# Layer 1's modulation with plain 4-byte products in place of split ones

## The chip, the cores and the metric

The kernel runs on one core of one Trainium2 chip. The metric is the device time of one launch, in microseconds (us): 5435.27 us is the median of three runs of the kernel before, which gave 5428.91, 5435.27 and 5438.29 us. Times inside the kernel come from one profiled execution of its own.

## What is computed

A backbone of two layers over 512 latent and 256 context tokens of width 1024. Each layer begins with a modulation: a conditioning vector (one for the latents, one for the context) is multiplied into a 1024 x 6144 weight matrix, and six vectors of 1024 (shift, scale and gate, twice) come out.

```python
cond_lat = jax.nn.silu(c)
cond_ctx = jax.nn.silu(c_ctx)
for l in range(DEPTH):
    mod_lat = (cond_lat @ w_mod[l] + b_mod[l])[:, None, :]
    mod_ctx = cond_ctx @ w_mod[l] + b_mod[l]
    sh1, sc1, gt1, sh2, sc2, gt2 = jnp.split(mod_lat, 6, axis=-1)
    h = _rmsnorm(x, g_norm1[l]) * (1.0 + sc1) + sh1
    p = h @ w_in[l]
    ...   # attention, short convolution, Hyena, merge, PEER experts
```

The Hyena branch needs a small filter network (two layers with sines) that depends on weights alone. Its first two steps are also computed during the modulation.

## The kernel before, in words

Every stage is a `Phase`: each engine has its own hand-written program, they meet through semaphores, and all engines wait for each other at the end of the stage. `phase_mod` (L764 to L919) is the stage of layer 1's modulation. It is the second stage of the program, after the load of the conditioning vectors, and nothing of another stage runs beside it. Layer 2's modulation is another function, `phase_mod_beside`, which runs beside the experts and which the diff leaves alone.

The weights come in 24 blocks of 1 MB, called halves here: 12 chunks of 512 output columns, each in two halves of 4 tiles of 128 rows (n counts halves, q = n // 2 counts chunks).

- **SyncE (SP)** issues the loads (L811) into a ring `raw` of 7 buffers. From the eighth on it first waits until VectorE has split half n - 7. Behind halves 7 to 10 it also issues the loads of x (2 MB), ctx (1 MB), rope and consts (L813).
- **ScalarE (ACT)** rounds each landed half to the reduced 4-byte format (`hi`, 3 buffers, L828). Between the halves it copies each finished chunk of 512 sums from PSUM into `rows` (`keep`, L822), sums the squares of the six token tiles at n = 16 to 21 (L837), takes their root at n = 23 (L841), and takes the two sines of the filter network at n = 12 and n = 23 (L761). The copy of the last chunk, `keep(11)`, stands behind the second sine.
- **VectorE (DVE)** computes the remainder `lo` = weights - `hi` (3 buffers, `split`, L265). At n = 3 and n = 14 it makes the filter network's angles (L727). At the end it normalises the tokens (`xn`, L911), adds the bias to the turned sums (L913) and forms the scales (L918).
- **TensorE (PE)** multiplies, for each half, 4 tiles of `hi` and 4 tiles of `lo` with `cond4`, the conditioning split in the same way into 4 columns (L873). After every second half it turns one kept chunk from 4 rows into 128 rows with 4 small products (`turn`, L861). At n = 2 and n = 13 it makes the filter network's products (L718). The last turn waits for `keep(11)`. At the end it transposes the modulation (L885), which ACT copies (L846) and SP stores (L801).
- **GpSimd (POOL)** reduces the filter network's angles to within pi in nine instructions each time (L742 to L755), and does nothing else in the stage.

The order inside each engine's program is what the loops over n write out; there is no planner.

Of the kernel before, what the change touches and what calls it, by code (L numbers as in the profile page):

```python
# [24 lines left out]
ALU = mybir.AluOpType  # L25
ACT = mybir.ActivationFunctionType
AX = mybir.AxisListType

P = 128
# [233 lines left out]
def split(nc, eng, hi, lo, x):  # L263

    return eng.tensor_tensor(lo, x, hi.bitcast(F32), ALU.subtract)  # L265
# [498 lines left out]
def phase_mod(c, layer, lay):  # L764
# [6 lines left out]

    nc, io = c.nc, c.io
    HALF = KD // 2
    RAW = 7
    chunks = 6 * D // 512
    raw = c.own(24, RAW, HALF * 512)
    DEEP = 3
    hi = [c.rounded(at, HALF * 512) for at in (80, 88, 96)]
    lo = [c.rounded(at, HALF * 512) for at in (140, 148, 192)]
    rows, turned_rows = c.at(178, 2, 512), c.at(178, 2, P)  # L780
    sel = c.at(182, 2)
    xn, junk = c.at(116, NT, D), c.at(184, 2, D)
    SQUARES = 16
    with Phase(nc) as ph:
# [3 lines left out]
                                    (c.rope[:], io["rope"]), (c.consts[:], io["consts"])]  # L788
        mlp = FilterMlp(c, ph, layer, T_ALL, lay.mlp_at)
        w_landed = [ph.sem(f"w_landed{s}") for s in range(RAW)]  # L790
        w_split, hi_ready, halves_done, kept, turned, cols_in, cond_split, dve_done = (ph.sem(s) for s in (
            "weights_split", "high_ready", "halves_done", "rows_kept", "rows_turned", "cols_landed",
            "cond_split", "dve_steps"))

        mod_ready, mod_turned, rows_made, rows_stored = (ph.sem(s) for s in (
            "mod_ready", "mod_turned", "rows_made", "rows_stored"))
# [1 line left out]
        def keep_rows(sp):  # L798
            sp.wait_ge(rows_made, 1)
            for s in range(2):  # L800
                sp.dma_start(c.mod_rows[layer][s], turned_rows[0:N_MOD, s]).then_inc(rows_stored, 16)  # L801
            sp.wait_ge(rows_stored, 32)

        @ph.block.sync
        def _(sp):
            sp.dma_start(c.cols[:], io["cols"][layer]).then_inc(cols_in, 16)
            mlp.sync(sp)
            for n in range(2 * chunks):
                if n >= RAW:
                    sp.wait_ge(w_split, n - RAW + 1)  # L810
                sp.dma_start(raw[:, n % RAW], io["w_mod"][layer][n]).then_inc(w_landed[n % RAW], 16)  # L811
                if n >= RAW and x_loads:
                    sp.dma_start(*x_loads.pop(0)).then_inc(x_in, 16)  # L813
            keep_rows(sp)

        @ph.block.scalar
        def _(act):
            def keep(q):
                act.wait_ge(halves_done, 2 * q + 2)
                if q >= 2:  # L820
                    act.wait_ge(turned, q - 1)
                nc.scalar.activation(rows[0:4, q % 2], c.bank(q % 2, 512, 4), ACT.Copy).then_inc(kept, 1)  # L822

            for n in range(2 * chunks):
                act.wait_ge(w_landed[n % RAW], 16 * (n // RAW + 1))
                if n >= DEEP:
                    act.wait_ge(halves_done, n - DEEP + 1)
                nc.scalar.activation(hi[n % DEEP], raw[:, n % RAW], ACT.Copy).then_inc(hi_ready, 1)  # L828
                if n >= 3 and n % 2:
                    keep((n - 3) // 2)  # L830
                if SQUARES <= n < SQUARES + NT:
                    t = n - SQUARES
                    if layer == 0 and t == 0:
                        act.wait_ge(x_in, 64)
                    if t >= 2:
                        act.wait_ge(sq, t - 1)
                    nc.scalar.activation(junk[:, t % 2], c.xs[:, t], ACT.Square,  # L837
                                         accum_out=c.stat[:, 0, t:t + 1]).then_inc(sq, 1)
                if n == SQUARES + NT + 1:
                    act.wait_ge(ms, 1)  # L840
                    nc.scalar.activation(c.stat[:, 1, 0:NT], c.stat[:, 1, 0:NT], ACT.Sqrt).then_inc(root, 1)  # L841
                if n in (12, 23):
                    mlp.scalar(act, n // 23, lay.hidden)
            keep(chunks - 1)
            act.wait_ge(mod_turned, 2)
            nc.scalar.activation(turned_rows[0:N_MOD], c.psum[0:N_MOD, 0:2 * P].rearrange("p (s q) -> p s q", s=2),  # L846
                                 ACT.Copy).then_inc(rows_made, 1)
# [7 lines left out]
        @ph.block.tensor  # L855
        def _(pe):
            def turn(q):
                pe.wait_ge(kept, q + 1)
                for j in range(4):
                    at = 7 * 512 + 8 * q + 2 * j  # L860
                    last = nc.tensor.matmul(c.psum[:, at:at + 2], rows[0:4, q % 2, j * P:(j + 1) * P], sel[0:4],  # L861
                                            start=True, stop=True)
                last.then_inc(turned, 1)

            pe.wait_ge(cond_split, 4)
            for n in range(2 * chunks):
                q, half = n // 2, n % 2
                if half == 0 and q >= 2:
                    pe.wait_ge(kept, q - 1)
                for part, ready in ((hi, hi_ready), (lo, w_split)):  # L870
                    pe.wait_ge(ready, n + 1)
                    for k in range(HALF):
                        last = nc.tensor.matmul(c.bank(q % 2, 512, 4), c.cond4[:, half * HALF + k],  # L873
                                                part[n % DEEP][:, k * 512:(k + 1) * 512],
                                                start=(half == 0 and part is hi and k == 0),
                                                stop=(half == 1 and part is lo and k == HALF - 1))
                last.then_inc(halves_done, 1)
                if n in (2, 13):
                    mlp.tensor(pe, n // 13)
                if n >= 3 and half:  # L880
                    turn((n - 3) // 2)
            turn(chunks - 1)
            pe.wait_ge(mod_ready, 2)
            for s in range(2):
                nc.tensor.transpose(c.psum[0:N_MOD, s * P:(s + 1) * P], c.mod[:, :, s], c.ident[:]).then_inc(mod_turned, 1)  # L885

        @ph.block.vector
        def _(dve):
            st = Steps(dve, dve_done)
            nc.vector.tensor_copy(c.cond4[:, :, 0:2], c.cond[:]).then_inc(cond_split, 1)  # L890
            dve.wait_ge(cond_split, 1)
            split(nc, nc.vector, c.cond4[:, :, 0:2], c.cond4[:, :, 2:4], c.cond[:]).then_inc(cond_split, 1)
            nc.vector.tensor_copy(sel[0:4], c.ident[0:4, 0:2]).then_inc(cond_split, 1)
            dve.wait_ge(cond_split, 3)
            nc.vector.tensor_tensor(sel[0:4], sel[0:4], c.ident[0:4, 2:4], ALU.add).then_inc(cond_split, 1)
            for n in range(2 * chunks):
                dve.wait_ge(hi_ready, n + 1)
                split(nc, nc.vector, hi[n % DEEP], lo[n % DEEP], raw[:, n % RAW]).then_inc(w_split, 1)
                if n == 3:
                    dve.wait_ge(cols_in, 16)  # L900
                if n in (3, 14):
                    mlp.vector(dve, n // 14)
                if n == SQUARES + NT:
                    dve.wait_ge(sq, NT)
                    nc.vector.tensor_scalar(c.stat[:, 1, 0:NT], c.stat[:, 0, 0:NT], 1.0 / D, EPS, ALU.mult,
                                            ALU.add).then_inc(ms, 1)
            dve.wait_ge(root, 1)
            st.do(nc.vector.reciprocal(c.stat[:, 0, 0:NT], c.stat[:, 1, 0:NT]))
            st.wait()
            for t in range(NT):  # L910
                nc.vector.tensor_scalar(xn[:, t], c.xs[:, t], c.stat[:, 0, t:t + 1], None, ALU.mult).then_inc(xn_ready, 1)  # L911
            dve.wait_ge(turned, chunks)
            st.do(nc.vector.tensor_tensor(  # L913
                c.mod[:], c.psum[:, 7 * 512:7 * 512 + 2 * N_MOD].rearrange("p (j s) -> p j s", s=2),
                c.cols[:, C_BMOD:C_BMOD + N_MOD].unsqueeze(2).to_broadcast([P, N_MOD, 2]), ALU.add))
            st.wait()
            for n, (sc, g) in enumerate(((SC1, C_G1), (SC2, C_G2))):
                nc.vector.scalar_tensor_tensor(  # L918
                    out=c.mod[:, sc:sc + KD] if n else c.ab[:], in0=c.mod[:, sc:sc + KD], scalar=1.0,  # L919
                    in1=c.cols[:, g:g + KD].unsqueeze(2).to_broadcast([P, KD, 2]), op0=ALU.add, op1=ALU.mult).then_inc(mod_ready, 1)  # L920
# [1919 lines left out]
```

## Time and profile before

| | |
|---|---|
| median of three runs | 5435.27 us |
| the profiled execution, its own time | 5433.36 us |
| its span, first to last instruction | 5431.3 us |
| mean granted TensorE clock over the span | 0.814 |
| busy share of the span: PE, DVE, POOL, ACT | 69%, 61%, 37%, 37% |
| the modulation stage of layer 1 in the span | 3.3 to 101.7 us |

The span is what the profile covers, from the first to the last instruction; the execution's own time is 2.1 us longer. A product of plain 4-byte operands shows up in the profile as two MATMUL records and two LDWEIGHTS records, one of reduced 4-byte operands as one of each. The granted clock is given as a share of 2.4 GHz: 1.00 is 2.4 GHz and 0.50 is 1.2 GHz.

### The profile page before, as it was taken

To read this page: it belongs to the slowest core of one execution; us is meant where nothing else is said; L and a number is where in the kernel's file an instruction comes from. 1 tells how busy PE (TensorE), PEld (TensorE's weight loads), DVE (VectorE), ACT (ScalarE), POOL (GpSimd) and SP (SyncE) were. 2 spreads that over 40 slices of the span, in tenths; PEclk is the share of its full clock that TensorE was granted. 3 is DMA by queue.
4 is the path that set the end of the run, shared out by engine and by line. 5 is a ranking of instruction groups with operands and counts; after the bars stand their busy time and mean duration, and the time that the engine had idled before them with its cause. 6 is when DMAs were issued, how large, how long until landed. Compare 5 with 4: busy or idle time off the path is not lost. (4 is left out here: it accounts for less than half of the span.)

```text
span 5431.3 us, 59703 instructions
## 1 busy us (share of the span) xinstructions
PE 3760.0 (69%) x19504; PEld 1838.0 (34%) x19504; DVE 3330.3 (61%) x7026; ACT 1988.8 (37%) x5136; POOL 2036.3 (37%) x1533
## 2 busy tenths in 40 slices
PE   6899879987565555555577679678976555555554
PEld 3677338876111111111122245246852111111111
DVE  7622452223777777777687777764135777777776
ACT  5432002212443344343354444325223443343443
POOL 5112003212444444444483356211434444444443
PEclk8999989998767777777688889889988777777777
DMA  5012002212999999999998989841327999999998
GB/s 237 16 44 70 4 16 65 63 67 103 400 418 410 416 410 417 415 414 414 378 363 349 367 327 375 349 171 37 98 80 325 421 412 417 413 415 416 411 417 345
DMA packets 230644, 1532.43 MB, mean 282 GB/s; under 512 B 26164, under 2 KB 26740, under 8 KB 58044
## 3 DMA queue, kind: packets, MB, share of 16 engines
q0 software_dynamic: 184320, 1342.26, 60.5%
q1 hardware_dynamic: 46012, 186.36, 9.4%
q8 instruction: 154, 2.52, 0.2%
q14 instruction: 158, 1.29, 0.1%
HBM read 1515.31 MB, written 13.21 MB: 281 GB/s over the span
## 5 line engine op out<-in xcount | busy, mean ns | idle before, releaser
L536 PE MATMUL psum<-arena 64*64 64x512 f32 x10240 | 1769.8, 825 | 1220.8 <-ACT arena L515 1209.6
L491 POOL DMA_INDIRECT arena<-in_uv,arena x1280 | 1462.9, 1143 | 1817.7 <-PE psum L536 1392.6
L651 DVE SCALAR_TENSOR_TENSOR arena<-arena 128x1024 f32<-128x1024 f32 x1280 | 1621.4, 1267 | 697.8 <-DMA arena<-in_uv,arena 653.0
L536 PEld LDWEIGHTS psum<-arena 64*64 64x64 f32 x10240 | 418.1, 169 | 2519.8 <-ACT arena L515 1892.9
L1549 PE MATMUL psum<-view_at,view_at 128*128 128x512 f32 (+1 forms) x4896 | 966.5, 359 | 19.1 <-PEq L165 10.3
L504 ACT ACTIVATE arena<-arena 128x1 f32<-128x1 f32 x1280 | 258.2, 202 | 1850.8 <-DVE arena L651 1811.0
L265 POOL TENSOR_TENSOR view_at<-view_at,view_at 128x1024 fp32r<-128x1024 f32 (+1 forms) x192 | 455.2, 2380 | 1238.7 <-ACT view_at L299 1208.4
L1549 PEld LDWEIGHTS psum<-view_at,view_at 128*128 128x128 f32 x4896 | 815.3, 191 | 185.2 <-issue 54.4
L515 ACT ACTIVATE arena<-arena 128x64 f32<-128x64 f32 x1280 | 445.1, 348 | 52.7 <-PE psum L536 10.9
L508 ACT ACTIVATE arena<-arena 128x1 f32<-128x1 f32 x1280 | 376.9, 294 | 46.7 <-ACT arena L504 0.4
L299 ACT ACTIVATE view_at<-view_at 128x1024 fp32r<-128x1024 f32 (+1 forms) x176 | 163.9, 939 | 330.6 <-DMA view_at<-in_w_in 188.2
L2405 DVE TENSOR_TENSOR view_at<-view_at,psum 128x768 f32<-128x768 f32 (+1 forms) x48 | 39.4, 821 | 376.2 <-PE psum L1549 376.2
L265 DVE TENSOR_TENSOR view_at<-view_at,view_at 128x2048 fp32r<-128x2048 f32 (+5 forms) x106 | 177.0, 1697 | 83.7 <-ACT view_at L2371 37.2
L2468 PE MATMUL psum<-view_at,view_at 128*128 128x512 f32 x480 | 114.5, 402 | 35.2 <-DVE view_at L265 34.1
L1269 PE MATMUL psum<-view_at,view_at 128*128 128x256 f32 (+1 forms) x528 | 96.7, 346 | 28.1 <-PEq L165 28.1
L2468 PEld LDWEIGHTS psum<-view_at,view_at 128*128 128x128 f32 x480 | 93.4, 195 | 56.0 <-issue 34.6
L504 ACT ACT_TABLE_LOAD x85 | 109.1, 1283 | 2.9 <-PEq L165 1.4
L1019 PE MATMUL psum<-view_at,cond 128*4 128x512 f32 x192 | 63.0, 466 | 64.8 <-POOL view_at L265 35.7
L651 DVE DVE_READ_ACCUMULATOR arena<-arena 128x1 f32 x1280 | 104.8, 82 | 0.0
L2240 PE MATMUL psum<-arena 128*128 128x256 f32 (+2 forms) x232 | 80.0, 511 | 34.6 <-DVE arena L2282 34.6
L558 DVE MAX8 arena<-arena 128x8 f32<-128x128 f32 (+1 forms) x240 | 81.5, 339 | 35.9 <-DVE arena L556 1.5
L472 ACT ACT_TABLE_LOAD x80 | 102.6, 1283 | 1.4
(246 smaller groups left out, 3445.6 us busy)
## 6 DMA issues: line engine op xcount, KB each, us to landing
view_at<-in_w_in SPq DMA_DIRECT2D x108, 512.0 KB, 6.6
view_at<-in_w_mod SPq DMA_DIRECT2D x48, 1024.0 KB, 12.9
arena<-in_uv,arena POOLq DMA_INDIRECT x1280
view_at<-in_w_br SPq DMA_DIRECT2D x48, 256.0 KB
view_at<-in_w_out SPq DMA_DIRECT2D x16, 512.0 KB, 8.7
view_at<-in_wq SPq DMA_DIRECT2D x16, 512.0 KB, 3.4
arena<-mod_rows SPq DMA_DIRECT2D x12, 512.0 KB
keep_spectrum<-arena SPq DMA_DIRECT2D x18, 256.0 KB, 6.9
```

The lines of the kernel that those rows point to most:

```text
L265: return eng.tensor_tensor(lo, x, hi.bitcast(F32), ALU.subtract)
L299: self._high(act, lambda out, x: self.c.nc.scalar.activation(out, x, ACT.Copy), n)
L472: self.c.nc.scalar.activation(self.exps[:, u % 2], self.topc, ACT.Exp, bias=self.small[:, u % 2, 0:1], accum_out=self.small[:, u % 2, 1:2] ...
L491: nc.gpsimd.indirect_dma_start(out=self.slots[i % self.ring], out_offset=None, in_=self.table, in_offset=bass.IndirectOffsetOnAxis(ap=self ...
L504: nc.scalar.activation(self.gelus[:, q, k:k + 1], self.dots[:, q, k:k + 1], ACT.Gelu).then_inc(self.act_steps, 1)
L508: nc.scalar.activation(self.scaled[:, q, k:k + 1], self.gelus[:, q, k:k + 1], ACT.Copy, scale=self.probs[:, q, k:k + 1]).then_inc(self.act ...
L515: nc.scalar.activation(self.diag[:, i % 4], self.ident2, ACT.Copy, scale=self.scaled[:, q, k:k + 1]).then_inc(self.diag_ready, 1)
L536: last = nc.tensor.matmul(self.c.psum[tokens, at:at + 512], self.diag[rows, k % 4], self.slots[k % self.ring][rows, D + h * 512:D + (h + 1 ...
L651: nc.vector.scalar_tensor_tensor(out=self.junk, in0=self.slots[i % self.ring][:, 0:D], scalar=1.0, in1=self.h2_turned if i % 2 else self.h ...
L1269: last = nc.tensor.matmul(out, h[:, k, at], m[:, lo:hi, k, :], start=(k == 0 and i == 0), stop=(k == KD - 1 and i == 2))
L1549: last = nc.tensor.matmul(c.psum[:, at + lo:at + hi], a[:, k], b[:, k, lo:hi], start=(k == 0 and i == 0), stop=(k == kt - 1 and i == 2))
L2468: last = nc.tensor.matmul(c.bank(2 * (t % 4) + h), a[:, k, t * P:(t + 1) * P], b[:, 4 * h:4 * h + 4, k, :], start=(k == 0 and i == 0), sto ...
```

## The change

The halves are no longer rounded and split. TensorE multiplies the landed 4-byte weights with the unsplit 4-byte conditioning, whose 2 columns replace the 4 of `cond4`. The ring is 10 buffers deep, SP waits for TensorE's products instead of VectorE's split, and the rows that are kept and turned are 2 instead of 4. The 48 instructions of rounding and splitting go away, as do the two that made `sel`. `cond4` is still made, for layer 2.

```diff
-    RAW = 7
+    RAW = 10
     chunks = 6 * D // 512
     raw = c.own(24, RAW, HALF * 512)
-    DEEP = 3
-    hi = [c.rounded(at, HALF * 512) for at in (80, 88, 96)]
-    lo = [c.rounded(at, HALF * 512) for at in (140, 148, 192)]
...
                 if n >= RAW:
-                    sp.wait_ge(w_split, n - RAW + 1)
+                    sp.wait_ge(halves_done, n - RAW + 1)
                 sp.dma_start(raw[:, n % RAW], io["w_mod"][layer][n]).then_inc(w_landed[n % RAW], 16)
...
-                nc.scalar.activation(rows[0:4, q % 2], c.bank(q % 2, 512, 4), ACT.Copy).then_inc(kept, 1)
+                nc.scalar.activation(rows[0:2, q % 2], c.bank(q % 2, 512, 2), ACT.Copy).then_inc(kept, 1)
 
             for n in range(2 * chunks):
-                act.wait_ge(w_landed[n % RAW], 16 * (n // RAW + 1))
-                if n >= DEEP:
-                    act.wait_ge(halves_done, n - DEEP + 1)
-                nc.scalar.activation(hi[n % DEEP], raw[:, n % RAW], ACT.Copy).then_inc(hi_ready, 1)
...
-                    last = nc.tensor.matmul(c.psum[:, at:at + 2], rows[0:4, q % 2, j * P:(j + 1) * P], sel[0:4],
+                    last = nc.tensor.matmul(c.psum[:, at:at + 2], rows[0:2, q % 2, j * P:(j + 1) * P], c.ident[0:2, 0:2],
                                             start=True, stop=True)
...
-            pe.wait_ge(cond_split, 4)
...
-                for part, ready in ((hi, hi_ready), (lo, w_split)):
-                    pe.wait_ge(ready, n + 1)
-                    for k in range(HALF):
-                        last = nc.tensor.matmul(c.bank(q % 2, 512, 4), c.cond4[:, half * HALF + k],
-                                                part[n % DEEP][:, k * 512:(k + 1) * 512],
-                                                start=(half == 0 and part is hi and k == 0),
-                                                stop=(half == 1 and part is lo and k == HALF - 1))
+                pe.wait_ge(w_landed[n % RAW], 16 * (n // RAW + 1))
+                for k in range(HALF):
+                    last = nc.tensor.matmul(c.bank(q % 2, 512, 2), c.cond[:, half * HALF + k], raw[:, n % RAW, k * 512:(k + 1) * 512],
+                                            start=(half == 0 and k == 0), stop=(half == 1 and k == HALF - 1))
                 last.then_inc(halves_done, 1)
...
             for n in range(2 * chunks):
-                dve.wait_ge(hi_ready, n + 1)
-                split(nc, nc.vector, hi[n % DEEP], lo[n % DEEP], raw[:, n % RAW]).then_inc(w_split, 1)
```

## Rows read from the trace of the kernel before

**Rows 1.** Groups of instructions by line, 0 to 110 us
```profile
L265 DVE TENSOR_TENSOR view_at<-view_at,view_at 128x2048 fp32r<-128x2048 f32 x24 | 58.8, 2472 | 21.5 <-ACT view_at L828 21.5
L873 PE MATMUL psum<-view_at,cond 128*4 128x512 f32 x192 | 54.2, 431 | 22.6 <-ACT view_at L828 15.7 <-DVE view_at L265 6.8
L828 ACT ACTIVATE view_at<-view_at 128x2048 fp32r<-128x2048 f32 x24 | 45.6, 1906 | 21.7 <-DMA view_at<-in_w_mod 20.9 <-PE psum L873 0.5
```

**Rows 2.** Busy time by stretch: PE, PEld, DVE, ACT, POOL, granted clock, DMA share, GB/s
```profile
10.00:35.00 25.00, 21.81 (x92) 8.55 (x92) 19.04 (x9) 16.76 (x12) 11.59 (x3) 1.00 1.01 425
35.00:52.00 17.00, 12.87 (x36) 4.30 (x36) 10.56 (x4) 10.47 (x7) 16.49 (x7) 0.60 1.01 417
52.00:76.00 24.00, 22.66 (x110) 9.97 (x109) 20.93 (x11) 21.97 (x22) 15.05 (x4) 1.00 0.95 395
76.00:94.00 18.00, 10.64 (x54) 4.74 (x53) 17.42 (x10) 10.81 (x13) 17.33 (x7) 0.95 0.00 0
```

**Rows 3.** Order of time, end of the stage: start, duration, engine, line
```profile
88.56 7.15 DVE L911 TENSOR_SCALAR arena<-arena,stat 128x1024 f32<-128x1024 f32 x6
...
93.87 0.84 ACT L761 ACTIVATE arena<-arena 64x768 f32<-64x768 f32 x1 [6.10 <-POOL arena L755]
94.62 0.57 ACT L822 ACTIVATE arena<-psum 4x512 f32<-4x512 f32 x1
...
95.25 1.86 PE L861 MATMUL psum<-arena 4*128 4x2 f32 x8 [4.69 <-ACT arena L822]
97.14 0.26 DVE L913 TENSOR_TENSOR mod<-psum,cols 128x96 f32<-128x96 f32 x1 [1.43 <-PE psum L861]
...
101.72 6.13 PE L1145 MATMUL psum<-ident,arena 128*128 128x128 f32 x36 [3.34 <-PEq L165]
```

**Rows 4.** GpSimd in order of time, the second reduction, first and last of nine
```profile
62.25 7.22 POOL L742 TENSOR_SCALAR arena<-arena 64x768 f32<-64x768 f32 x1 [8.78 <-DVE arena L727]
...
92.69 1.15 POOL L755 TENSOR_SCALAR arena<-arena 64x768 f32<-64x768 f32 x1
```

**Rows 5.** Order of time, 8 to 18 us: the first half arrives
```profile
10.22 1.91 ACT L828 ACTIVATE view_at<-view_at 128x2048 fp32r<-128x2048 f32 x1 [7.56 <-DMA view_at<-in_w_mod]
...
12.67 1.91 ACT L828 ACTIVATE view_at<-view_at 128x2048 fp32r<-128x2048 f32 x1 [0.54 <-DMA view_at<-in_w_mod]
...
17.03 0.12 PEld L873 LDWEIGHTS psum<-view_at,cond 128*4 128x4 f32 x1 [0.30 <-issue]
...
17.31 0.55 PEld L873 LDWEIGHTS psum<-view_at,cond 128*4 128x4 f32 x3 [0.15 <-issue]
```

**Rows 6.** TensorE and its weight loads at 574 us: plain 4-byte products, one stationary column
```profile
574.26 3.59 PE L1964 MATMUL psum<-arena,consts 128*1 128x512 f32 x8
...
575.97 0.08 PEld L1964 LDWEIGHTS psum<-arena,consts 128*1 128x1 f32 x1 [0.34 <-issue]
576.40 0.08 PEld L1964 LDWEIGHTS psum<-arena,consts 128*1 128x1 f32 x1 [0.35 <-issue]
```

**Rows 7.** TensorE at 521 us: a stretch that begins at the lower clock
```profile
521.44 3.33 PE L218 MATMUL psum<-ones,ident 128*128 128x128 f32 x14 [7.09 <-PEq L165]
525.26 7.16 PE L1945 MATMUL psum<-arena 64*128 64x512 f32 x8 [0.49 <-DMA arena<-in_hy_w]
```

**Rows 8.** Busy time by stretch, at and after the stretch of rows 7
```profile
527.00:533.00 6.00, 6.00 (x8) 2.16 (x7) 1.76 (x2) 3.57 (x5) 0.00 (x0) 0.50 0.96 412
536.00:540.00 4.00, 4.00 (x10) 1.50 (x10) 1.22 (x1) 0.70 (x1) 0.00 (x0) 1.00 0.02 8
```

**Rows 9.** TensorE in order of time, 59 to 71 us: halves, a filter product, turns
```profile
59.56 1.50 PE L718 MATMUL psum<-arena 64*64 64x512 f32 x4
60.99 1.05 PE L861 MATMUL psum<-arena 4*128 4x2 f32 x8
61.97 3.86 PE L873 MATMUL psum<-view_at,cond 128*4 128x512 f32 x16
...
66.74 3.86 PE L873 MATMUL psum<-view_at,cond 128*4 128x512 f32 x16
```

More of the change, by code:

```diff
@@ L773, in phase_mod @@
     HALF = KD // 2
-    RAW = 7
+    RAW = 10
     chunks = 6 * D // 512
     raw = c.own(24, RAW, HALF * 512)
-    DEEP = 3
-    hi = [c.rounded(at, HALF * 512) for at in (80, 88, 96)]
-    lo = [c.rounded(at, HALF * 512) for at in (140, 148, 192)]
     rows, turned_rows = c.at(178, 2, 512), c.at(178, 2, P)
-    sel = c.at(182, 2)
     xn, junk = c.at(116, NT, D), c.at(184, 2, D)
@@ L790, in phase_mod @@
         w_landed = [ph.sem(f"w_landed{s}") for s in range(RAW)]
-        w_split, hi_ready, halves_done, kept, turned, cols_in, cond_split, dve_done = (ph.sem(s) for s in (
-            "weights_split", "high_ready", "halves_done", "rows_kept", "rows_turned", "cols_landed",
-            "cond_split", "dve_steps"))
+        halves_done, kept, turned, cols_in, dve_done, cond_split = (ph.sem(s) for s in (
+            "halves_done", "rows_kept", "rows_turned", "cols_landed", "dve_steps", "cond_split"))
         mod_ready, mod_turned, rows_made, rows_stored = (ph.sem(s) for s in (
@@ L892, in _ @@
             split(nc, nc.vector, c.cond4[:, :, 0:2], c.cond4[:, :, 2:4], c.cond[:]).then_inc(cond_split, 1)
-            nc.vector.tensor_copy(sel[0:4], c.ident[0:4, 0:2]).then_inc(cond_split, 1)
-            dve.wait_ge(cond_split, 3)
-            nc.vector.tensor_tensor(sel[0:4], sel[0:4], c.ident[0:4, 2:4], ALU.add).then_inc(cond_split, 1)
             for n in range(2 * chunks):
-                dve.wait_ge(hi_ready, n + 1)
-                split(nc, nc.vector, hi[n % DEEP], lo[n % DEEP], raw[:, n % RAW]).then_inc(w_split, 1)
                 if n == 3:
```

## The prediction

> **What bounds the kernel now.** The change touches one stage, from 3.3 to 101.7 us of the span, so I read that stretch alone. The grouped lines come first [rows 1]: VectorE's 24 splits are busy 58.8 us, TensorE's 192 products 54.2 us, ScalarE's 24 roundings 45.6 us. None fills the stage's 98 us, so the table by stretch says who is ahead when [rows 2]. Until 76 us the DMA share is 0.95 to 1.01 at 395 to 425 GB/s: the transfers pace the stage, and the engines keep up but for a dip of TensorE, with a granted clock of 0.60, between 35 and 52 us. From 76 us on nothing moves (DMA 0.00), and VectorE (17.42 of 18 us) and GpSimd (17.33 of 18 us) are busy. So the last 18 us aren't the weights' transfer.
>
> The order of time at the end shows who closes the stage [rows 3]. ScalarE's second sine (L761) starts at 93.87 us, after waiting 6.10 us for GpSimd's last angle. Behind it stand the copy of the last chunk (94.62), the last turn on TensorE (95.25, 1.86 us long), the bias (97.14), and the next stage at 101.72. GpSimd's second reduction runs from 62.25 to 93.84 us, 31.6 us in nine instructions [rows 4]. The stage ends by this chain: weights until half 13, filter product, VectorE's angles, 31.6 us of GpSimd, sine, last chunk.
>
> **The change, part by part, and its sum.**
>
> What is removed: 58.8 us of VectorE and 45.6 us of ScalarE. Neither is worth anything by itself beyond the chain above: it is worth at most 101.7 us less the length of what takes its place. What takes its place is TensorE's stream, because a plain product costs more there.
>
> Price of a plain product. The profile has plain 4-byte products with 512 moving columns and a single stationary column: eight records in 3.59 us, weight loads 0.43 us apart (575.97 to 576.40) [rows 6]. Each product makes two records, so a product is 0.86 us and a half of four is 3.44 us. Two columns instead of one should cost the same; now a half is eight reduced records, 16 of them (two halves) in 3.86 us [rows 9], so 1.93 us. The step is from 1.93 to 3.44 us for each half, and a half arrives every 2.45 us (roundings of the first two halves start at 10.22 and 12.67 [rows 5], each waiting for a load). TensorE thus changes from faster than the transfers to slower than them.
>
> The Trainium skill, "Perfetto Trace Analysis", section "Engine Utilization", halves the array's output rate for FP32_LOW_HIGH. Taken for the whole product this would be 0.43 us a product, half the price that rows 6 show; taken for each record it agrees with them. The first reading is the faster rival below.
>
> Sum, in times of the span:
> - First product: the first half has landed at 10.2 us [rows 5]; today TensorE waits for the rounding, in future it doesn't.
> - 24 halves x 8 records x 0.43 us = 82.6 us.
> - Half rate at the begin. At 17.03 us a weight load still comes 0.42 us after the one before it (0.12 long, 0.30 idle), at 17.31 the idle time falls to 0.15 [rows 5]: the records go from 0.42 to some 0.24 us, so they ran at 1.2 GHz before, although the column says 1.00 there [rows 2]. That is 5 us after the first product, which follows the first rounding (10.22 + 1.91 = 12.1 us). Five microseconds at half rate lose 2.5 us. The other bound is the stretch at 521 us: TensorE begins at 521.44, a record still takes 0.9 us at 525 to 532 us (8 in 7.16), clock 0.50, and it is at 1.00 in the window from 536 [rows 7, 8]. Some 14.5 us, a loss of 7.2. I take 2.5, since that is this very stage with all 128 rows in use, where rows 7 have 64.
> - Ten turns before the last half ends. From a turn to the next product 0.98 us (60.99 to 61.97); from the pair's period, 4.77 us (61.97 to 66.74) less 3.86, it is at least 0.91 [rows 9]. With the tail of the last record under the turn I take 1.06: 10.6 us. Two rows instead of four change nothing: the cost is eight weight loads and eight tiny records.
> - Two filter products: 59.56 to 60.99, 1.43 us, with the gap ahead 1.5: 3.0 us.
> - Sum: 10.2 + 82.6 + 2.5 + 10.6 + 3.0 = 108.9; the copy of the last chunk starts at 109.1, against 94.62 today.
> - From that copy to the next stage today 101.72 - 94.62 = 7.1 us, of which the last turn is 1.86 at the low clock; on a TensorE just busy it is 1.05 [rows 3, 9]. So 6.3 us: next stage at 115.4, which is 13.7 us later.
> - The next stage starts with 36 transposes in 6.13 us at the lower clock [rows 3]. After a dense stream they may start fast. The first eight release VectorE, after which it is busy: between 0 and 2 us gained, I take 0.5.
>
> Together +13.2 us.
>
> What has to stay hidden. **Transfers:** half n needs its load by 10.2 + 2.5 + about 4.1 n us (3.44 and half a turn), and the queue delivers 1 MB in 2.45 us plus 3.1 MB of x, ctx, rope, consts (7.7 us) once; ten buffers hold 34 us of products, so SP's new wait for `halves_done` is never on the path. Behind it on SP stand only further loads. **GpSimd:** second filter product after half 13 at about 69 us, angles at 71, and even with today's 31.6 us [rows 4] it ends at 102.5. Without the splits beside it I expect it shorter. ScalarE comes to the second sine only after `keep(10)`, which needs half 21 (101) and the root, about 103.5; sine and tables end near 105.5, before 109. The first reduction has from 26 to 58 us even at 31.6 us, and TensorE asks for it behind half 13, at 67. **VectorE:** the root comes at 103.3 instead of 88, since it stands behind `keep(10)`; then the 7.15 us of `xn` [rows 3] end at 110.8, and the bias could start at 110.9. This is a tie: 0 to 0.5 us late.
>
> The profiled execution took 5433.36 us, so the changed kernel's would take 5446.6. The median of the runs, 5435.27 us, is 1.9 us higher; against it I forecast 5448.5 us. TensorE becomes the bound of the stage.
>
> **Rivals.**
> 1. No measurable change (chance 0.29). A measurement of this kernel can tell about 0.2%, 11 us, from no change, and the forecast is only 2 us above that. A quicker rise of the clock (loss 1 instead of 2.5), 2 us from transposes that start fast, or turns at 0.91 us (1.5 less) bring +8 to +11, some 5445. For it: the scatter of the three runs is 9 us. Against: these are small terms on 82.6 us that no view lets shrink.
> 2. Faster (0.07). If the two records of a product overlapped or were one for two columns, a half would cost 1.72 us, less than a load takes, and the transfers would pace the stage: half 13 lands at about 50, GpSimd runs from 55 to 86.5 at the old pace, the last copy starts at about 87.4 instead of 94.62. That with the warm turn is -8; with GpSimd freed of the splits up to -12, where `xn` closes the stage. Time about 5425. It decides below 2.5 us a half. Rows 6 with one column speak against it.
> 3. Much slower (0.04). If plain products with 2 of 128 columns don't hold TensorE at 2.4 GHz, each record is 0.86 us or more [rows 7]: the stream costs twice 82.6, turns 1.86 each, some +100 us, 5536. Rows 6 are eight records at the full rate, too short a burst to exclude it wholly; today's four columns do hold it [rows 2, 9].
> 4. The loads run dry in spite of the ring, as between 35 and 52 us today [rows 2]. At 2.45 us for a load against 3.44 for a half there is no way for it; it would only add to the forecast's side. I give it nothing of its own.
>
> **How the numbers follow.** Forecast (slower by over 0.2%) 0.60, rival 1 0.29, rival 2 0.07, rival 3 0.04. Slower is 0.60 + 0.04 = 0.64, same 0.29, faster 0.07. The range: down, quicker clock 1.5, transposes 1.5, turns 1.5, not all at once, and 4 us of run scatter give 5440; up, the 14.5 us rise (+4.7), the tie 0.5 and the same scatter give 5458. It leaves out rivals 2 and 3.
>
> **What the changed profile would show.** No 128x2048 instructions before 100 us on VectorE and ScalarE; L873's successor with 192 records, about 0.58 us each (3.59 less seven times 0.43 [rows 6]) and 0.43 us apart; TensorE without a gap over 1 us from 10.2 to about 109; the DMA share falling before 80 us or stretching as SP waits for TensorE; GpSimd's nine instructions in well under 31.6 us; the last copy on ScalarE waiting for TensorE, not sitting behind the sine; the next stage at about 115. Wrong would be a half in less than 2.5 us, or a granted clock of 0.50 in the middle of the stream, or a sine that starts after 109.

## The result and the profile after

The changed kernel takes 5451.23 us in the median of eight runs, the kernel before 5437.64 in the median of eight. The ratio is 1.0026 with a 95% interval of [1.0018, 1.0035], so the change costs 10 to 19 us. The forecast was +13.2 us against the median then shown (5448.5 from 5435.27); the measured difference of the medians is +13.6. That the two agree to 0.4 us is partly luck, since the interval is 9 us wide.

| | before | after |
|---|---|---|
| median of eight runs | 5437.64 us | 5451.23 us |
| profiled execution, own time | 5433.36 us | 5452.62 us |
| span | 5431.3 us | 5450.6 us |
| first product of the modulation | 12.28 us | 10.17 us |
| last chunk's copy (`keep(11)`) | 94.62 us | 109.16 us |
| first TensorE record of the next stage | 101.72 us | 115.60 us |

The grouped lines of the kernel after, 0 to 130 us (line, engine, operation, shapes, count | busy us, mean ns | idle before and its releaser), answer to [rows 1]:

```profile
L862 PE MATMUL psum<-view_at,cond 128*2 128x512 f32 x192 | 87.1, 608 | 10.2 <-DMA view_at<-in_w_mod 10.2
L749 POOL TENSOR_SCALAR arena<-arena 64x768 f32<-64x768 f32 x6 | 12.8, 2125 | 0.5
L742 POOL TENSOR_SCALAR arena<-arena 64x768 f32<-64x768 f32 x2 | 1.7, 827 | 52.9 <-DVE arena L727 52.9
L893 DVE TENSOR_SCALAR arena<-arena,stat 128x1024 f32<-128x1024 f32 x6 | 4.1, 749 | 0.0
```

There are still 192 records on TensorE, but they are busy 87.1 us instead of 54.2, and TensorE waits once, 10.2 us for the first load. The 24 roundings and the 24 splits are gone. The table by stretch of the kernel after (PE, PEld, DVE, ACT, POOL, granted clock, DMA share, GB/s) answers to [rows 2]:

```profile
16.00:35.00 19.00, 19.00 (x52) 4.48 (x51) 1.07 (x1) 1.17 (x2) 8.58 (x5) 1.00 1.03 430
35.00:52.00 17.00, 17.00 (x51) 4.56 (x49) 0.00 (x0) 1.17 (x2) 6.99 (x5) 1.00 1.00 413
52.00:76.00 24.00, 24.00 (x75) 7.07 (x75) 1.07 (x1) 3.53 (x6) 5.12 (x4) 1.00 0.95 394
76.00:94.00 18.00, 18.00 (x60) 5.39 (x58) 0.00 (x0) 6.04 (x12) 10.43 (x6) 1.00 0.00 1
```

TensorE is busy in every microsecond of these four stretches, at the full clock, also from 35 to 52 us where it had fallen to 0.60. The transfers end near 76 us as before; TensorE then has another 33 us to do. The order of time at the end of the stage answers to [rows 3]:

```profile
93.18 1.05 PE L852 MATMUL psum<-ident,arena 2*128 2x2 f32 x8
...
94.16 7.03 PE L862 MATMUL psum<-view_at,cond 128*2 128x512 f32 x16
...
101.12 1.05 PE L852 MATMUL psum<-ident,arena 2*128 2x2 f32 x8
...
103.59 4.07 DVE L893 TENSOR_SCALAR arena<-arena,stat 128x1024 f32<-128x1024 f32 x6
104.64 0.84 ACT L761 ACTIVATE arena<-arena 64x768 f32<-64x768 f32 x1
109.06 1.94 PE L852 MATMUL psum<-ident,arena 2*128 2x2 f32 x16
109.16 0.59 ACT L817 ACTIVATE arena<-psum 2x512 f32<-2x512 f32 x1 [3.67 <-PE psum L862]
111.04 0.26 DVE L895 TENSOR_TENSOR mod<-psum,cols 128x96 f32<-128x96 f32 x1 [3.38 <-PE psum L852]
...
115.60 7.01 PE L1127 MATMUL psum<-ident,arena 128*128 128x128 f32 x36 [3.33 <-PEq L165]
```

A pair of halves with its turn takes 7.94 us (93.18 to 101.12), where it took 4.77 [rows 9]. The sine (L761) is done at 105.5, and the last copy now waits 3.67 us for TensorE, not for GpSimd. The stage ends 13.9 us later (115.60 less 101.72).

The profiled span is 19.3 us longer, more than the stage explains. The rows of one large group in both kernels (minimum, median and maximum ns of one; first and last start in us), before and after, show where the rest is:

```profile
L1549 PE MATMUL psum<-view_at,view_at x4896: 277/389/793, 306.7 to 4098.6; 128*128 128x512 f32 x130, 128*128 128x256 f32 x66
```

```profile
L1531 PE MATMUL psum<-view_at,view_at x4896: 277/389/794, 318.7 to 4114.4; 128*128 128x512 f32 x130, 128*128 128x256 f32 x66
```

The shift is 12.0 us at 307 us of the span, 15.8 at 4099 and 19.3 at the end. The diff touches nothing there, and the eight runs of one kernel lie 13 to 16 us apart (5442.83 to 5455.65 after, 5428.91 to 5444.51 before). I read 5.4 of the 19.3 us as that scatter, which no single profile can resolve; the medians, 13.6 us apart, agree with the stage's 13.9.

### The profile page after: what moved, and what is told of

The parts are those of the page before. It is cut to its first block and busy times, and to the rows that moved or that the text cites. A ratio compares the mean times of both kernels' runs of the same rounds, so it can differ in the third digit from the quotient of the medians.

```text
span 5450.6 us, 59631 instructions
## 1 busy us (share of the span) xinstructions
PE 3781.2 (69%) x19504; PEld 1828.9 (34%) x19504; DVE 3266.7 (60%) x7000; ACT 1946.9 (36%) x5112; POOL 2009.3 (37%) x1533
## 3 DMA queue, kind: packets, MB, share of 16 engines
HBM read 1515.31 MB, written 13.21 MB: 280 GB/s over the span
## 5 line engine op out<-in xcount | busy, mean ns | idle before, releaser
L265 DVE TENSOR_TENSOR view_at<-view_at,view_at 128x512 fp32r<-128x512 f32 (+5 forms) x82 | 117.7, 1464 | 63.2 <-ACT view_at L2353 37.6
L504 ACT ACT_TABLE_LOAD x85 | 109.1, 1283 | 2.9 <-PEq L165 1.5
```

The costliest lines, as they stand in the source:

```text
L504: nc.scalar.activation(self.gelus[:, q, k:k + 1], self.dots[:, q, k:k + 1], ACT.Gelu).then_inc(self.act_steps, 1)
```

## The experiments

The landmark in all of them is the first TensorE record of the next stage: 101.72 us before, 115.60 after. Each kernel was profiled once, so how far the landmark scatters isn't measured in itself; the runs below give a measure. The first 24 records of the modulation took 13.21 us in the changed kernel and 11.99 in run 3, whose begin is the same. So a difference of about a microsecond between two landmarks tells nothing, where the whole time scatters by ten. The runs were made at four times, on three chips; each time the kernel before ran too, and whole times are compared only with that one.

**1. Half the products.** `for k in range(HALF)` becomes `for k in (0, HALF - 1)`; tiles 1 and 2 of each half are left out of the sums.

> The changed kernel with two of the four products of each half left out (tiles 1 and 2 of each half don't enter the sums). Theory, TensorE's stream sets the stage: the records go from 192 to 96, 41 us of stream go away, and the transfers take over: last half landed at about 75.5 us, root and xn behind it, next stage at about 86 us of the span instead of 115.6, some 29 us less in all (about 5422 us). Rival, the stage is held by latencies between the engines or by ScalarE's and VectorE's tail: the next stage stays above 105 us.

The order of time at the end of its stage:

```profile
74.38 1.88 PE L862 MATMUL psum<-view_at,cond 128*2 128x512 f32 x4
...
76.52 1.88 PE L862 MATMUL psum<-view_at,cond 128*2 128x512 f32 x4 [0.26 <-DMA view_at<-in_w_mod]
...
84.87 3.44 PE L1127 MATMUL psum<-ident,arena 128*128 128x128 f32 x15 [3.33 <-PEq L165]
```

The next stage starts at 84.87 us, 30.7 earlier (86 was expected), and now TensorE waits for the last load. So the stream set the stage, and the transfers stand behind it, 31 us lower. The whole took 5412.66 us, the kernel before beside it 5424.29, one run each.

**2. Five products instead of four.** The loop becomes `for k in (0, 1, 1, 2, 3)`; tile 1 enters the sums twice.

> The changed kernel with tile 1 of each half multiplied twice (it enters the sums twice), five products instead of four. Theory, TensorE's stream sets the stage at 0.86 us a product: 24 x 0.86 = 20.6 us more, next stage at 136 us. Rival, there is slack beside the stream: less than 10 us more.

```profile
135.48 0.87 PE L1127 MATMUL psum<-ident,arena 128*128 128x128 f32 x3 [3.33 <-PEq L165]
```

That is the first row of its next stage: 19.9 us later for 24 more products, 0.83 us each (0.86 expected, 20.6 in all). Of the missing 0.7 us 0.6 lie in a shorter stretch at half rate at the begin: its first 30 records took 15.17 us, where 13.21 us and six records of 0.43 make 15.79. There is no slack beside the stream. The whole took 5462.77 us against 5424.29.

**3. A ring of 3.** `RAW = 10` becomes `RAW = 3`.

> The changed kernel with a ring of 3 buffers instead of 10. Theory, the depth is worth nothing because a half of products (3.44 us) takes longer than a load (2.45 us): next stage at 115.6 to 118, with at most 3 us of waiting where the 2 MB of x pass between two halves. Rival, the ten buffers are what carries the change: TensorE waits for loads all through, 10 us more or above.

The first row is of its table by stretch, 16 to 35 us, the second the begin of its next stage:

```profile
16.00:35.00 19.00, 18.09 (x49) 4.22 (x48) 1.07 (x1) 1.17 (x2) 9.65 (x6) 1.00 1.00 401
```

```profile
115.24 1.09 PE L1127 MATMUL psum<-ident,arena 128*128 128x128 f32 x4 [3.25 <-PEq L165]
```

TensorE misses 0.9 us in the stretch where the load of x passes, and the next stage starts at 115.24, where it was 115.60 with ten. That doesn't make the depth worthless: this execution had a shorter stretch at half rate at the begin (its records are 0.43 us apart from 13.5 us on, the changed kernel's from 15.9), and its first 24 records were done at 22.2 us instead of 23.4. The 1.2 us won there shrink to 0.4 at the next stage, so three buffers cost 0.8 us, which is the wait. Ten buffers buy no more than that once a half takes longer than a load. The whole took 5430.15 us against 5424.29.

**4. Warmed.** `c.warm_up(ph, pe, 14, bank=6)` stands ahead of TensorE's loop.

> The changed kernel with 14 products of 128x128 ahead of the first half, in the 6.8 us in which TensorE waits for it. Theory, the first records run at half rate because TensorE was idle, and that costs 2.5 to 3 us: the weight loads are 0.43 us apart from the first half on, next stage 2.5 to 3 us earlier, at 113. Rival, the half rate has another cause (the first loads, the clock column's 1.00): the first seven records stay 0.85 us apart and nothing is gained.

TensorE's first weight loads in the changed kernel, and then in this one:

```profile
10.97 0.13 PEld L862 LDWEIGHTS psum<-view_at,cond 128*2 128x2 f32 x1 [0.72 <-issue]
11.83 0.13 PEld L862 LDWEIGHTS psum<-view_at,cond 128*2 128x2 f32 x1 [0.72 <-issue]
...
15.91 0.09 PEld L862 LDWEIGHTS psum<-view_at,cond 128*2 128x2 f32 x1 [0.54 <-issue]
16.34 0.09 PEld L862 LDWEIGHTS psum<-view_at,cond 128*2 128x2 f32 x1 [0.34 <-issue]
```

```profile
3.25 4.92 PE L218 MATMUL psum<-ones,ident 128*128 128x128 f32 x28 [3.25 <-PEq L165]
...
10.73 0.08 PEld L863 LDWEIGHTS psum<-view_at,cond 128*2 128x2 f32 x1 [0.35 <-issue]
11.16 0.08 PEld L863 LDWEIGHTS psum<-view_at,cond 128*2 128x2 f32 x1 [0.35 <-issue]
...
112.97 1.30 PE L1128 MATMUL psum<-ident,arena 128*128 128x128 f32 x5 [3.31 <-PEq L165]
```

Unwarmed, the records are 0.86 us apart until about 15.5 us and 0.43 after; warmed, they are 0.43 us apart from the first. The next stage starts at 112.97, 2.6 us earlier: that is the price of the half rate at the begin in the profiled execution of the changed kernel, 2.5 in the sum. It isn't the same each time: against 24 records at the full rate (7.03 us for 16 and 0.43 for each further one, 10.47 in all) the changed kernel loses 2.7 us, and run 3 1.5. The whole took 5440.45 us against 5424.29, one run each, and tells nothing about 2.6 us.

**5 and 6. What bounded the kernel before.** Run 5 is the kernel before without VectorE's splits; TensorE multiplies `hi` twice and SP waits for `hi_ready`. Run 6 keeps the splits and cuts GpSimd's nine instructions to the ninth, so that angles are clipped at pi instead of reduced.

> The kernel before with VectorE's 24 splits left out; TensorE multiplies the rounded half twice, so the remainders don't enter the sums and the products are as many as before. Theory, the splits slow GpSimd and its two reductions close the stage: a reduction falls from 31.6 to about 16.3 us (as in the changed kernel), the last copy waits for TensorE, next stage at 86 to 89 us instead of 101.7. Rival, the reductions aren't what closes the stage or don't depend on the splits: next stage stays above 97.

> The kernel before with GpSimd's reductions cut to their ninth instruction (the angles are clipped at pi, not reduced), the splits all there. Theory, GpSimd's chain closes the stage and costs the splits time too: splits back at 2.29 us each from 2.47 in the mean, next stage at 86 to 89 us. Rival, VectorE's splits are themselves what the stage waits for: next stage above 95.

From the grouped lines and the order of time of run 5:

```profile
L742 POOL TENSOR_SCALAR arena<-arena 64x768 f32<-64x768 f32 x2 | 1.7, 828 | 40.6 <-DVE arena L727 40.6
L749 POOL TENSOR_SCALAR arena<-arena 64x768 f32<-64x768 f32 x6 | 12.8, 2127 | 0.5
...
81.91 1.28 ACT L841 ACT_TABLE_LOAD   x1
...
85.48 0.57 ACT L822 ACTIVATE arena<-psum 4x512 f32<-4x512 f32 x1
...
92.31 6.23 PE L1143 MATMUL psum<-ident,arena 128*128 128x128 f32 x36 [3.34 <-PEq L165]
```

And of run 6:

```profile
L265 DVE TENSOR_TENSOR view_at<-view_at,view_at 128x2048 fp32r<-128x2048 f32 x24 | 54.5, 2287 | 23.0 <-ACT view_at L828 22.8
...
93.22 6.79 PE L1145 MATMUL psum<-ident,arena 128*128 128x128 f32 x36 [3.34 <-PEq L165]
```

Without splits the nine instructions are as short as in the changed kernel: the first of them takes 0.83 us, where it took 7.22 in the second reduction [rows 4]. With one GpSimd instruction left in place of nine a split is 2.29 us, from 2.47. In both the stage ends 8.5 to 9.4 us earlier than before. So GpSimd's chain did close the stage, and the two engines slowed each other. But 86 to 89 us was expected and 92 to 93 came: a second limit stands close behind. In run 5 it is ScalarE's tail: from 81.91 to 85.48 us it loads two tables and takes root and sine before the last copy. The normalisation ends at 87.74 us there, level with the last turn (87.70). In run 6 the splits, the last of which begins at 82.25, and the normalisation behind them come last. The whole took 5416.46 and 5419.05 us, one run each, beside 5429.3, the median of 13 runs of the kernel before.

The Trainium skill, "SBUF — State Buffer", section "SBUF: two separate sides", says that VectorE and GpSimd share a pair of ports, and that of an instruction of VectorE with two inputs in SBUF and one of GpSimd that reads SBUF the one that starts first has the pair for its whole length, while the other is blocked. The trace agrees that one is blocked: a split has two inputs, and the same nine instructions beside ScalarE and TensorE alone are undisturbed. It also shows for how long. In the kernel before VectorE makes three splits without a gap, and in run 6 the one GpSimd instruction left meets three as well:

```profile
62.09 6.68 DVE L265 TENSOR_TENSOR view_at<-view_at,view_at 128x2048 fp32r<-128x2048 f32 x3
```

```profile
60.39 6.68 DVE L265 TENSOR_TENSOR view_at<-view_at,view_at 128x2048 fp32r<-128x2048 f32 x3
60.55 7.21 POOL L853 TENSOR_SCALAR arena<-arena 64x768 f32<-64x768 f32 x1 [27.80 <-DVE arena L727]
```

The GpSimd instruction that starts beside them (62.25 us, 7.22 long [rows 4], and 60.55 us, 7.21 long) ends 0.7 us after the last of the three, so it waits for the whole row of splits and not for one. In run 6 the splits lose nothing by this waiting.

**7 to 10. Mixed forms.** A plain half costs TensorE 1.5 us more but frees VectorE and ScalarE, and so GpSimd. These kernels make some chunks plain and split the others, with the ring of 7:

```diff
+    PLAIN = (2, 3, 7, 8)
+    split_n = [n for n in range(2 * chunks) if n // 2 not in PLAIN]
...
+                if n not in split_n:
+                    pe.wait_ge(w_landed[n % RAW], 16 * (n // RAW + 1))
+                    for k in range(HALF):
+                        last = nc.tensor.matmul(c.bank(q % 2, 512, 2), c.cond[:, half * HALF + k], raw[:, n % RAW, k * 512:(k + 1) * 512],
+                                                start=(half == 0 and k == 0), stop=(half == 1 and k == HALF - 1))
```

Run 8 adds the 14 warming products and `SQUARES = 13`; run 9 has `PLAIN = (2, 7)` and `SQUARES = 13` without warming; run 10 has `PLAIN = (0, 2, 7)`, the warming and `SQUARES = 13`.

> A mixed form: chunks 2, 3, 7 and 8 (8 of 24 halves) as in the changed kernel, the other 16 split as before, ring of 7. The plain chunks stand where GpSimd reduces the angles. Theory: TensorE's stream is 16 halves of 1.85 us and 8 of 3.44, with turns and filter products some 76 us from 12.1 us on, GpSimd is free of most splits; next stage at 90 to 95 us, before both kernels (101.7 and 115.6). Rival: GpSimd is still slowed by the splits left or TensorE waits for them between the plain chunks: next stage at 98 or later.

> The mixed form of the run before it, with the 14 warming products ahead and the sums of squares three halves earlier (n = 13 to 18), so that root and normalisation don't stand at the end. Theory: 2 to 3 us less than without, next stage at 88 to 92 us, so 10 to 13 us less than the kernel before in the whole (5424 to 5428 on the chip of the first runs, a ratio of 0.998). Rival: the stage's gain is given back by the next ones, whose loads start with them: no measurable difference.

> The mixed form with only chunks 2 and 7 plain (4 of 24 halves), the squares three halves earlier as in the run before, no warming. In that run TensorE was busy without a gap from 52 us to the end, so the four plain halves of chunks 3 and 8 were too many: each costs 1.6 us more there than a split one. Theory: 6.4 us less on TensorE, VectorE's 20 splits just fit; next stage at 89 to 92 us, 10 to 13 us less than the kernel before in the stage, a ratio of 0.998 in the whole. Rival: GpSimd, slowed by the splits that come back, or VectorE itself is late: next stage at 95 or later, no measurable difference.

> As the run before it, with chunk 0 plain too and the 14 warming products ahead of it. A plain first half can start at 10.2 us at the full rate (as the warmed run showed), where a split one starts at 12.1. Theory: TensorE loses nothing by it and VectorE has two splits less: next stage at 87 to 91 us, ratio 0.998 or a little below. Rival: nothing gained over the run before it, since VectorE isn't late there: the two within 1 us of each other.

| run | plain chunks | next stage at, us | ratio to before, 95% interval |
|---|---|---|---|
| 7 | 2, 3, 7, 8 | 97.43 | one run: 5428.29 us against 5429.3 |
| 8 | 2, 3, 7, 8, warmed | 95.43 | 0.9996 [0.9987, 1.0006] |
| 9 | 2, 7 | 99.98 | 0.9996 [0.9987, 1.0005] |
| 10 | 0, 2, 7, warmed | 99.51 | 0.9995 [0.9985, 1.0004] |

All four start the next stage earlier than the kernel before, by 1.7 to 6.3 us, none as early as expected, and none can be told from it in the whole. The rival of run 8, that the next stages give the gain back, isn't borne out: the first product of the large group shown above, at 306.7 us in the kernel before, comes 6.9, 6.9, 3.3 and 2.2 us earlier in the four. The gains are just smaller than what the whole time can tell. In run 8 TensorE was busy without a gap from 52 us to the end, so I took plain halves away, and got worse. The order of time of run 9, in which splits come back, shows what closed the stage:

```profile
77.46 4.05 POOL L749 TENSOR_SCALAR arena<-arena 64x768 f32<-64x768 f32 x1
...
80.15 11.15 DVE L265 TENSOR_TENSOR view_at<-view_at,view_at 128x2048 fp32r<-128x2048 f32 x4
...
84.20 2.75 POOL L755 TENSOR_SCALAR arena<-arena 64x768 f32<-64x768 f32 x1
...
91.43 4.07 DVE L928 TENSOR_SCALAR arena<-arena,stat 128x1024 f32<-128x1024 f32 x6
95.42 0.25 DVE L930 TENSOR_TENSOR mod<-psum,cols 128x96 f32<-128x96 f32 x1
```

Four splits take 11.15 us, 2.79 each, and a GpSimd instruction 4.05 where it takes 2.12 alone; the normalisation stands behind the last split and closes the stage. The rival came true. The slower splits explain some 4 of the 8 us by which the expectation was missed (in run 11 four take 9.07 us; two more took 6.60 us from 72.92 on); ahead of these VectorE had waited 4.24 us for ScalarE's rounding. Run 10 shows the same: its four splits take 11.16 us, and its next stage starts 0.5 us before that of run 9, so its rival, nothing gained, came true too, though VectorE was late, against what the rival assumed. Run 8's warming was lost: its first half is split and its first product comes 3.7 us after the warming ends, with the records 0.42 us apart again, the reduced product's half rate.

**11 and 12. The angles on VectorE.** The eighteen instructions move from GpSimd to VectorE, at the place where the angles are made, ahead of the splits that wait behind a plain chunk.

```diff
-        @ph.block.gpsimd
-        def _(pool):
-            for i in range(2):
-                for _ in mlp.gpsimd(pool, i):
-                    pass
...
                     mlp.vector(dve, n // 14)
+                    for _ in mlp.gpsimd(dve, n // 14, nc.vector):
+                        pass
```

> The mixed form with chunks 2 and 7 plain, and the eighteen instructions that reduce the angles on VectorE instead of GpSimd, while TensorE multiplies the plain chunk behind them. No GpSimd work is left in the stage. Theory: the pair of GpSimd's reads and VectorE's splits slowed both in the runs before (splits up to 4 us, GpSimd's last instruction at 86.9 us); apart from each other a split is 2.29 us and a reduction some 6 to 8 us on VectorE, hidden behind 6.9 us of plain products. Next stage at 87 to 91 us, 11 to 15 us less than before, ratio 0.9975. Rival: VectorE's reductions are late for the splits of the next chunk and TensorE waits for them: next stage above 94.

> As the run before it, with chunks 0 and 11 plain too and the 14 warming products. Chunk 11 plain takes rounding and split out of the path behind the last load. Theory: TensorE is then ahead of neither loads nor splits by much, last half done at about 83 us, next stage at 87 to 91 us. Rival: the 6.4 us that four more plain halves cost TensorE aren't covered: 2 us or more above the run before it.

Run 11 in order of time: VectorE's first reduction, first and last instruction, and the end of the stage.

```profile
22.98 0.55 DVE L743 TENSOR_SCALAR arena<-arena 64x768 f32<-64x768 f32 x1
...
28.86 0.55 DVE L756 TENSOR_SCALAR arena<-arena 64x768 f32<-64x768 f32 x1
...
85.13 4.07 DVE L925 TENSOR_SCALAR arena<-arena,stat 128x1024 f32<-128x1024 f32 x6
...
89.11 0.25 DVE L927 TENSOR_TENSOR mod<-psum,cols 128x96 f32<-128x96 f32 x1
...
93.46 5.98 PE L1159 MATMUL psum<-ident,arena 128*128 128x128 f32 x36 [3.33 <-PEq L165]
```

And its splits in the grouped lines:

```profile
L265 DVE TENSOR_TENSOR view_at<-view_at,view_at 128x2048 fp32r<-128x2048 f32 x20 | 45.4, 2288 | 17.9 <-ACT view_at L837 17.8
```

A reduction takes 6.4 us on VectorE (22.98 to 29.41) instead of 31.6 on GpSimd beside the splits [rows 4], and each split is back at 2.29 us. The next stage starts at 93.46, 8.3 us earlier than before (87 to 91 expected): the normalisation, which VectorE makes behind its last split, ends at 89.2 and closes the stage. In the whole run 11 takes 5416.39 us in the median, the kernel before beside it 5424.04, ratio 0.9989 [0.9980, 0.9998]. This is the one version of the five measured in this way whose interval lies below the kernel before (and so below the changed kernel, which is above it); the gain is 1 to 11 us, near the limit of what can be told. Run 9 differs from it only by the place of the eighteen instructions, so these are worth 6.5 us of the stage (99.98 less 93.46). Whether the plain chunks are needed for that isn't shown: the kernel before with the angles on VectorE and all halves split wasn't run. Run 12, with chunks 0 and 11 plain too, starts the next stage at 96.21 us and has a ratio of 0.9995 [0.9986, 1.0004]: its last chunk holds TensorE from 82.91 to 89.9. Its rival came true.

## Why the prediction was right

**The bound before.** GpSimd's reductions as the last link were right (runs 5 and 6). That the stage would then be free to fall by 13 to 16 us, which I expected of those runs, was wrong: ScalarE's tail and VectorE's normalisation stood 8.5 to 9.4 us behind. The prediction didn't rest on that.

**The price of a plain product.** 0.43 us a record, two records a product: it came as said, also with two columns (0.34 idle and 0.09 long between weight loads), and run 2 measured 0.83 us a product in the stage. The reading of the Trainium skill's "Perfetto Trace Analysis", section "Engine Utilization", by which a whole product would cost 0.43 us, is excluded; each record alone agrees with it.

**The sum.** First product at 10.17 (10.2 said). Half rate at the begin 2.6 us (2.5 said), which run 4 took away. The last copy at 109.16 (109.1 said). From the copy to the next stage 6.44 us (6.3 said). The next stage at 115.60 (115.4 said). That the half rate agrees to 0.1 us is luck, since other runs lost 1.5 and 2.1 us there (runs 3 and 2). A turn cost 0.91 us beyond 7.03 of products in a pair of 7.94, where I counted 1.06 beyond 6.88: the same sum.

**The cover.** Loads, ScalarE and VectorE stayed hidden, and the ring's depth was worth 0.8 us at most (run 3). Two terms were on the safe side: I let GpSimd keep its 31.6 us, and it took 16.2 (70.64 to 86.85 us); I let `xn` keep 7.15 us and saw a tie with the last turn, and it took 4.07 and had 3.38 us to spare. Both had been slowed by the other engine, as runs 5 and 6 show.

**The term that was wrong.** Of the 0.5 us that the next stage's transposes should gain from a warm TensorE nothing came. They took 7.01 us instead of 6.13 [rows 3]. TensorE idles 3.33 us at the stage's border, and although its clock was 1.00 until 111 us, it is at 0.50 when the transposes begin, as before. The rows of one microsecond each in which it comes back (engines, granted clock and transfers as in the table by stretch), before and after:

```profile
105.00:106.00 1.00, 1.00 (x7) 1.00 (x6) 1.00 (x3) 0.85 (x1) 0.00 (x0) 0.58 1.04 340
```

```profile
121.00:122.00 1.00, 1.00 (x8) 1.00 (x7) 1.00 (x1) 0.84 (x1) 1.00 (x1) 0.73 0.96 373
```

That is some 4 us behind the first transpose before and 6 us after. Why it came back later stays open; runs 5 and 11, with 6.23 and 5.98 us, lie near the kernel before. It changed nothing behind them: VectorE's first instruction of that stage is 1.13 us behind the first transpose in both kernels.

**Two slips in the working.** The lower end of the range is called "not all at once", but 5440 is 5448.5 less all three terms of 1.5 us and less the 4 us of scatter. And a half with half a turn is 3.97 us (half of 7.94), not about 4.1, so the loads were needed a little sooner than was said. Neither touches the forecast.

**The rivals.** No measurable change was close: the interval's lower end, 1.0018, lies just under the 0.2% that I had named. The faster and the much slower case are excluded by the record spacing and by a clock of 1.00 in every stretch from 16 to 109 us.

## What to carry to other kernels

Removing work from two engines is worth no more than the gap to the stream that takes its place: here 104 us of rounding and splitting went, 33 us of TensorE came, and the stage ended 13.9 us later. Count a product's records and their spacing before trading split reduced products for plain ones, and compare the price of a block with the price of its load: below it the loads set the time (run 1), above it every further product shows (run 2). And where GpSimd and VectorE work in the same stage, ask how long each instruction takes alone; in the mixed form, moving 18 small GpSimd instructions to VectorE gave what no mixture of products did.

## What the runs showed of the hardware that I had not expected

- A GpSimd instruction of 64x768 elements (L742) takes 0.83 us alone and took 7.2 and 9.4 us beside three and four back-to-back splits of 128x2048, ending 0.7 us after the last of them; a whole reduction of nine took 16.2 us alone, 31.6 beside splits, and 6.4 us on VectorE.
- VectorE's single-input instructions were slowed too: the six of `xn` took 7.15 us beside GpSimd and 4.07 alone.
- 28 small records ahead of the first load kept TensorE at the full rate over an idle time of 1.3, 2.0 and 2.1 us (runs 10, 12 and 4). Over 3.7 us they did not (run 8), where the first half's records were back at 0.42 us for a product that takes 0.24 at the full rate, and the granted clock from 12 to 17 us was 0.50.
- Without warming, the changed kernel's TensorE came to the full rate at about 15.5 us, 5.3 us after its first product; in runs 2 and 3, with the same begin, it came there at about 14.8 and 13.4 us. The granted-clock column reads 1.00 over that stretch; only the spacing of the records shows the half rate.
